# x laid out turned for the first projection, its first slab worked unit by unit over three row tiles, x's rows loaded from GpSimd's queue

## The chip, the cores and the metric

The kernel runs on one core of a Trainium2 chip. A core has TensorE (PE in the profile), VectorE (DVE), ScalarE (ACT), GpSimd (POOL) and the sync engine (SP), each with its own instruction order, and 16 DMA engines that they share. The metric is the device time of one execution in microseconds (us); lower is better.

## What is computed

Two transformer blocks follow each other on x of 512 rows and 1024 columns, all in float32. Only the head of the first block matters here:

```python
xn = rmsnorm(x, attn_norm_g)                  # x / sqrt(mean(x*x) + eps) * g, by row
proj = jnp.einsum('bsd,de->bse', xn, w_in)    # 512 x 1024 times 1024 x 2312
qa, ka, va, qb, kb, vb, f_logit = jnp.split(proj, IN_SPLITS, axis=-1)
qa = rmsnorm(qa.reshape(b, s, A_HEADS, HEAD_DIM), q_norm_a)    # each head of 64 on its own
ka = rmsnorm(ka.reshape(b, s, A_KV_HEADS, HEAD_DIM), k_norm_a)
out_a = swa_sinks_attention(qa, ka, va, sink_logits)
...
log_f = jax.nn.log_sigmoid(f_logit + b_forget)
out_b = forgetting_attention(qb, kb, vb, log_f)
mixed = jnp.concatenate([out_a, out_b], axis=-1)
x = x + mixed @ w_out
x = x + jnp.square(jax.nn.relu(rmsnorm(x, mlp_norm_g) @ w_up)) @ w_down
```

The second block (modulated norms, neighbourhood attention, a pooling mixer, another MLP) comes after it and is not touched.

## The kernel before, in words

Every float32 product is made of three TensorE passes in a rounded format: each operand is split into a high part (ScalarE copies it, `w_hi`, `xt_hi`) and the rest (VectorE subtracts, `w_lo`, `xt_lo`), and hi*hi, hi*lo and lo*hi are summed in PSUM. Weights come in slabs of 1024 rows and up to 512 columns, each slab as four units `raw[0]` to `raw[3]` of 256 rows (512 KB at full width). The sync engine loads the units in order (`unit`, `slab`). The next slab's unit q waits until VectorE has split the present one (`unit_split`). `w_hi` and `w_lo` have two slots.

x is in four row tiles m of 128 rows. A product needs x turned, with the 1024 columns on the partitions (`xt_hi`, `xt_lo`, eight k-steps). Before the change row tile m is made so: its rows are loaded (512 KB), ScalarE squares and sums them (`first_squares`) and takes part of the root (`first_root`), VectorE refines the root (`refine`), multiplies the rows by root and gain (`scaled`), TensorE turns them against the identity matrix (`turn_rows`), ScalarE and VectorE split the result (`xt_high`, `xt_low`). Row tile 0 is multiplied by the gain alone, and its root is applied behind the product (`root0`, `late_root`). The gain's row is spread over the partitions by two small products with a row of ones.

`FIRST` is the order of the first eight output tiles g: slab 0 (q of the first attention) for row tiles 0, 1, 2, then slab 1 (k, v and the forget gates, 264 columns) for row tiles 0 to 3, then slab 0 for row tile 3. Tile g is in PSUM bank g % 4. A tile of q or k goes through a chain in which two engines alternate, one tile after the other: ScalarE squares it (`head_squares`), VectorE sums by head (`head_means`), ScalarE takes logarithm and exponential (`head_roots`), VectorE refines and multiplies (`head_rows`, into `qn`; it ends with `gemm_free`, which frees the bank), TensorE turns it (`turn_heads`), and ScalarE stores it with its gain (`head_gain`, into `q_a` or `k_a`, ends with `qk_stored`). In ScalarE's order the four units of slab 2 are split amid the chain of tiles 6 and 7.

Behind tile 7 TensorE makes the first scores (`scores(0)`), which wait for `gemm_free` 6 and `qk_stored` 4, and then tile 8 in pieces of three k-steps (`part_product`), which waits for `gemm_free` 7. From there on, attention and the tiles of slabs 2 to 4 alternate in a written-out order of 70 halves. Everything is ordered by semaphores whose counts are written into the code.

Of the kernel before, what the change touches and what calls it, by code (L numbers as in the profile page):

```python
# [14 lines left out]
P = 128  # L15
D = 1024
# [33 lines left out]
FIRST = ((0, 0), (0, 1), (0, 2), (1, 0), (1, 1), (1, 2), (1, 3), (0, 3))  # L50
N_IN1, N_OUT, N_MLP, N_IN2 = 5, 2, 4 * NCH, 4
# [188 lines left out]
def build(nc, t, out):  # L240
    ctx = ExitStack()
    with ctx:
# [50 lines left out]
        gain_row = at("gain_row", [1, D], F32, H + 28 * K)  # L293
        ones_row = at("ones_row", [1, P], F32, H + 20 * K)
# [37 lines left out]
        gains = place("gains", [P, 4], F32)  # L332
        cvec = place("cvec", [P, 2, KT], F32)
# [14 lines left out]
        gain1 = at("gain1", [P, D], F32, E)  # L348
# [38 lines left out]
        def sem(name):  # L387
# [15 lines left out]
        hi_split, unit_split = sem("hi_split"), sem("unit_split")  # L403
        gemm_done, gemm_free = sem("gemm_done"), sem("gemm_free")
# [10 lines left out]
        row_ready, gain_spread, gain_copied, first_half, gain_copied_act = (sem(n) for n in (  # L415
            "row_ready", "gain_spread", "gain_copied", "first_half", "gain_copied_act"))
# [34 lines left out]
        root0 = st[:, 3, STAT_N1:STAT_N1 + 1]  # L451

        def late_root(m):
            return {"scale": root0} if m == 0 else {}
# [3 lines left out]
        def _(sp):  # L458
            def small(dst, src, s):
                sp.dma_start(dst, src).then_inc(s, 16)  # L460

            def x_tile(m):
                sp.dma_start(x[:, m, :], t["x"][m * P:(m + 1) * P, :]).then_inc(x_loaded[m], 16)

            x_tile(0)
# [10 lines left out]
            def slab(s, w, c0, width):  # L476
                for q in range(UQ):
                    wait = 4 * (s - 1) + q + 1 if s else None
                    unit(q, rows(w, 0, q)[:, :, c0:c0 + width], width, wait)
                    if s == 0 and q == 0:  # L480
                        small(ident[:], t["c_ident"], ident_loaded)
                    if s == 0 and q:
                        x_tile(q)

            for s, (c0, width) in enumerate(IN1_COLS):
                if s == 1:

                    small_loads = (
                        (gains[0:HD, 0:1], t["q_norm_a"].rearrange("(p a) -> p a", a=1), heads_loaded),
                        (gains[HD:P, 0:1], t["q_norm_a"].rearrange("(p a) -> p a", a=1), heads_loaded),  # L490
                        (gains[0:HD, 1:2], t["k_norm_a"].rearrange("(p a) -> p a", a=1), heads_loaded),
                        (gains[HD:P, 1:2], t["k_norm_a"].rearrange("(p a) -> p a", a=1), heads_loaded),
                        (gains[0:HD, 2:3], t["q_norm_b"].rearrange("(p a) -> p a", a=1), heads_loaded),
                        (gains[HD:P, 2:3], t["q_norm_b"].rearrange("(p a) -> p a", a=1), heads_loaded),
                        (gains[0:HD, 3:4], t["k_norm_b"].rearrange("(p a) -> p a", a=1), heads_loaded),
                        (gains[HD:P, 3:4], t["k_norm_b"].rearrange("(p a) -> p a", a=1), heads_loaded),
                        (b_f[:], t["b_forget"].rearrange("(p a) -> p a", a=1), vec_loaded),
                        (sink[:], t["sink_logits"].rearrange("(a n) -> a n", a=1), vec_loaded),
                        (cvec[:, 0, :], t["c"], vec_loaded),
                        (cvec[:, 1, :], t["c_ctx"], vec_loaded),  # L500
                        (identb[:], t["c_identb"], vec_loaded),
                        (causal[:], t["c_causal"], vec_loaded),
                        (edge[:], t["c_edge"], vec_loaded),
                        (pscale[:], t["pool_scale"], vec_loaded),
                        (negsel[:].rearrange("h g p -> h (g p)"), t["c_negsel"], negsel_loaded),
                    )
                    for q in range(UQ):
                        src = rows(t["w_in"], 0, q)
                        for args in small_loads[5 * q:5 * (q + 1)]:
                            small(*args)  # L510
                        sp.wait_ge(unit_split, q + 1)
                        sp.dma_start(raw[q][:, :, 0:256], src[:, :, c0:c0 + 256]).then_inc(raw_loaded[q], 16)
                        sp.dma_start(raw[q][:, :, 256:KV_W], src[:, :, 2304:2312]).then_inc(raw_loaded[q], 16)
                else:
                    slab(s, t["w_in"], c0, width)
# [40 lines left out]
        def _(pool):  # L556
# [4 lines left out]

            pool.wait_ge(unit_split, 4 * (SLAB_OUT2 + 1))
# [21 lines left out]
        def _(act):  # L584
# [15 lines left out]
            load(gain_row[:], t["attn_norm_g"].rearrange("(a n) -> a n", a=1), gain1_loaded)  # L600
# [42 lines left out]
            first_squares(0)  # L643
            high_of(0, 0)
            first_root(STAT_N1)
            xt_high(NT_1, 0, halves=[0])
            high_of(0, 1)
            xt_high(NT_1, 0, halves=[1])
            first_squares(1)
            high_of(0, 2)  # L650
            act.wait_ge(gain_spread, 2)
            did(act.activation(gain1[:, NC:D], gp[3][:], ACT.Copy), gain_copied_act)
            first_root(STAT_N1 + 1)
            high_of(0, 3)
# [11 lines left out]
            def head_squares(g):  # L666
# [6 lines left out]
                if g == 0:  # L673
                    act.wait_ge(rs_done, 4)
                did(act.activation(qsq[:, 0:heads * HD], banks[in_bank(g)][:, 0:heads * HD], ACT.Square,
                                   **late_root(m)), hsq_done)
# [8 lines left out]
            first_squares(2)  # L685
            xt_high(NT_1 + 1, 1)
            first_root(STAT_N1 + 2)
            high_of(1, 0)
            high_of(1, 1)
            first_squares(3)  # L690
            head_squares(0)
            xt_high(NT_1 + 2, 2)
            first_root(STAT_N1 + 3)
            head_roots(0)
            high_of(1, 2)
            high_of(1, 3)
            xt_high(NT_1 + 3, 3)
            head_squares(1)
            head_roots(1)

            act.wait_ge(xr_ready, 4)
            load(alibi[:], t["c_alibi"], alibi_loaded)

            act.wait_ge(heads_loaded, 16 * 8)

            for g, (s, m) in list(enumerate(FIRST))[2:]:
                if g >= 3:
                    head_gain(g - 3)
# [8 lines left out]
                if s == 1:  # L717
                    did(act.activation(v_a[:, m, :], gp[g % 4][:, P:2 * P], ACT.Copy, **late_root(m)), v_copied)
# [361 lines left out]
        def _(pe):  # L1080
# [1364 lines left out]
```

## Time and profile before

| | before |
|---|---|
| median of 3 runs | 1186.05 us (1185.82 to 1186.39) |
| the profiled execution, its own time | 1186.4 us |
| its span in the trace | 1184.5 us |
| TensorE busy | 1167.0 us (99%) |
| VectorE, ScalarE, GpSimd busy | 706.3, 476.1, 24.8 us |
| mean granted TensorE clock | 0.998 |
| DMA | 144.28 MB, mean 122 GB/s |

All times in the trace count from the start of the span. TensorE's busy time is nearly the whole span, so the views of the first 55 us say more than the shares: there the timeline gives each instruction's start and length, and what the engine had waited for. A matmul is shown about 0.39 us long for 512 columns, while the next starts 0.23 us later: they are pipelined.

### The profile page before, as it was taken

The numbers are of one execution on the slowest core, as the hardware profiler recorded it, in microseconds if no ns is written. First come the engines' busy times: TensorE is split into PE (matmuls) and PEld (weight loads), VectorE is DVE, ScalarE is ACT, GpSimd is POOL, SyncE is SP. The second block draws the span as 40 slices with busy tenths as digits, with TensorE's granted clock in tenths as the row PEclk, the third lists the DMA queues.
The fourth block names the chain that finished last, engine by engine and source line by source line (L and its number), as shares of the span: only waits on it lengthen the run. The fifth ranks groups of instructions, "written<-read, shape, count | busy, mean of one in ns | idle before, by whom it ended". The sixth has DMA issues, their size and how long they took to land.

```text
span 1184.5 us, 16596 instructions
## 1 busy us (share of the span) xinstructions
PE 1167.0 (99%) x6158; PEld 946.1 (80%) x6160; DVE 706.3 (60%) x1084; ACT 476.1 (40%) x858; POOL 24.8 (2%) x23
## 2 busy tenths in 40 slices
PE   8999999989999999999999999999999999999997
PEld 5877776688888888888888886678988888888886
DVE  7786567768787786842788235747633333324335
ACT  6655344545234234324541114845631532432431
POOL 0000000000000000000000004300000000000000
PEclk9999999999999999999999999999999999999999
DMA  7322211218766676734425111222333322323301
GB/s 229 125 72 71 72 36 54 73 52 271 243 224 242 215 254 206 232 125 142 143 72 171 72 72 46 80 101 72 128 99 96 105 91 89 110 85 99 117 16 71
DMA packets 77533, 144.28 MB, mean 122 GB/s; under 512 B 8339, under 2 KB 12307, under 8 KB 77460
## 3 DMA queue, kind: packets, MB, share of 16 engines
q1 hardware_dynamic: 54882, 99.12, 24.7%
q10 hardware_dynamic: 22578, 44.18, 11.4%
q8 instruction: 46, 0.75, 0.3%
q14 instruction: 27, 0.22, 0.1%
HBM read 140.36 MB, written 2.13 MB: 120 GB/s over the span
## 4 chain that ended last, share of the span: by engine, by line
PE 91%; DVE 5%; ACT 2%; issue 2%; DMA 0%; DVEq 0%; ACTq 0%
PE gemm L1091 26%; PE gemm L1093 25%; PE gemm L1092 25%; PE aux L1132 1%; PE aux L1338 1%; PE gemm L1378 1%; PE gemm L1380 1%; PE gemm L1379 1%; DVE nmax L2199 1%; PE aux L1091 1%; PE gemm L1275 1%; PE aux L1093 1%; PE aux L1092 1%; PE gemm L1288 1%; PE aux L1617 1%
## 5 line engine op out<-in xcount | busy, mean ns | idle before, releaser
L1091 PE MATMUL gemm<-xt_hi,w_hi 128*128 128x512 f32 (+1 forms) x704 | 254.4, 361 | 1.3 <-issue 1.1
L1093 PE MATMUL gemm<-xt_hi,w_lo 128*128 128x512 f32 (+1 forms) x704 | 253.6, 360 | 0.0
L1092 PE MATMUL gemm<-xt_lo,w_hi 128*128 128x512 f32 (+1 forms) x704 | 253.5, 360 | 0.0
L1707 DVE TENSOR_TENSOR w_lo<-w_raw,w_hi 128x1024 fp32r<-128x1024 f32 (+1 forms) x176 | 208.0, 1210 | 35.1 <-ACT w_hi L842 30.4
L842 ACT ACTIVATE w_hi<-w_raw 128x1024 fp32r<-128x1024 f32 x124 | 124.1, 1050 | 211.4 <-PE gemm L1093 132.9
L1091 PE MATMUL gemm<-w_hi,ht_hi 128*128 128x512 f32 (+1 forms) x512 | 198.9, 388 | 0.0
L1093 PE MATMUL gemm<-w_hi,ht_lo 128*128 128x512 f32 (+1 forms) x512 | 198.4, 387 | 0.0
L1092 PE MATMUL gemm<-w_lo,ht_hi 128*128 128x512 f32 (+1 forms) x512 | 198.4, 387 | 0.0
L1091 PEld LDWEIGHTS gemm<-xt_hi,w_hi 128*128 128x128 f32 x704 | 132.7, 188 | 21.9 <-issue 1.7
L1093 PEld LDWEIGHTS gemm<-xt_hi,w_lo 128*128 128x128 f32 x704 | 132.7, 189 | 20.1
L1092 PEld LDWEIGHTS gemm<-xt_lo,w_hi 128*128 128x128 f32 x704 | 132.7, 188 | 19.8
L2005 DVE TENSOR_TENSOR ht_lo<-hid,ht_hi 128x512 fp32r<-128x512 f32 x64 | 44.3, 692 | 162.4 <-ACT hid L855 162.4
L1093 PEld LDWEIGHTS gemm<-w_hi,ht_lo 128*128 128x128 f32 x512 | 96.1, 188 | 19.7
L1092 PEld LDWEIGHTS gemm<-w_lo,ht_hi 128*128 128x128 f32 x512 | 96.2, 188 | 19.5
L1091 PEld LDWEIGHTS gemm<-w_hi,ht_hi 128*128 128x128 f32 x512 | 96.1, 188 | 19.4
L850 ACT ACTIVATE relu<-gemm 128x512 f32<-128x512 f32 x64 | 38.2, 597 | 165.3 <-PE gemm L1093 160.2
L2062 DVE SCALAR_TENSOR_TENSOR mod_acc<-wm,csil,mod_acc 128x512 f32<-128x512 f32 x112 | 84.1, 751 | 5.8 <-DMA wm<-in_w_mod 1.5
L1091 PE MATMUL gemm<-w_hi,xt_hi 128*128 128x512 f32 (+1 forms) x208 | 80.2, 386 | 0.4 <-DVE xt_lo L1697 0.4
L1093 PE MATMUL gemm<-w_hi,xt_lo 128*128 128x512 f32 (+1 forms) x208 | 77.9, 374 | 0.0
L1092 PE MATMUL gemm<-w_lo,xt_hi 128*128 128x512 f32 (+1 forms) x208 | 77.6, 373 | 0.0
L606 ACT ACTIVATE w_hi<-w_raw 128x1024 fp32r<-128x1024 f32 (+1 forms) x52 | 51.0, 1021 | 61.1 <-PE gemm L1093 60.0
L2019 DVE TENSOR_TENSOR sub<-sub,gemm 128x512 f32<-128x512 f32 (+1 forms) x24 | 16.2, 676 | 60.5 <-PE gemm L1093 60.5
(268 smaller groups left out, 1385.8 us busy)
## 6 DMA issues: line engine op xcount, KB each, us to landing
wm<-in_w_mod ACTq DMA_DIRECT2D x64, 512.0 KB, 4.7
w_raw<-in_w_in SPq DMA_DIRECT2D x32, 512.0 KB, 4.3
w_raw<-in_w_up SPq DMA_DIRECT2D x32, 512.0 KB, 3.9
w_raw<-in_w_down SPq DMA_DIRECT2D x32, 512.0 KB, 5.7
w_raw<-in_w_mlp_in SPq DMA_DIRECT2D x32, 512.0 KB, 3.6
w_raw<-in_w_mlp_out SPq DMA_DIRECT2D x32, 512.0 KB, 4.4
w_raw<-in_w_out SPq DMA_DIRECT2D x16, 512.0 KB, 4.0
x<-in_x SPq DMA_DIRECT2D x4, 512.0 KB, 6.5
```

The source lines that it names most:

```text
L606: act.activation(w_hi[slot(s)][:, UK * q:UK * (q + 1), 0:width], raw[q][:, :, 0:width], ACT.Copy).then_inc(hi_split, 1)
L842: act.activation(w_hi[s % 2][:, UK * q:UK * (q + 1), :], raw[q][:, :, :], ACT.Copy).then_inc(hi_split, 1)
L850: act.activation(relu[c % 2][:], gp[(t0 + c) % 4][:], ACT.Relu).then_inc(relu_done, 1)
L1091: pe.matmul(bank, lh, rh, start=(k == 0), stop=False)
L1092: pe.matmul(bank, lh, rl, start=False, stop=False)
L1093: mm = pe.matmul(bank, ll, rh, start=False, stop=(k == KT - 1))
L1132: mm = pe.transpose(dst, src, ident[:])
L1275: pe.matmul(bank[e][:, lo:256], q_a[rows[e], h // 2, n * P:(n + 1) * P], k_a[rows[e], swap, (n - 1) * P + lo:(n + 1) * P], start=True, sto ...
L1707: dve.tensor_tensor(w_lo[slot(s)][:, ks, 0:width], raw[q][:, :, 0:width], w_hi[slot(s)][:, ks, 0:width].bitcast(F32), ALU.subtract).then_i ...
L2005: dve.tensor_tensor(ht_lo[:, c, :], hid[c % 2][:], ht_hi[:, c, :].bitcast(F32), ALU.subtract).then_inc(hid_lo, 1)
L2019: dve.tensor_tensor(cols, cols, bank[:], ALU.add).then_inc(gemm_free, 1)
L2062: ins = dve.scalar_tensor_tensor(acc, w, c, acc, ALU.mult, ALU.add)
```

## The change

x is given to the kernel a second time, laid out turned (`x_turned`, 128 partitions, 8 k-steps, 512 tokens), and the gain with it by partition. ScalarE's queue loads it in five transfers, ScalarE makes `xt_hi` straight from it (`x_high`: a copy with the gain as scale, all four row tiles at once) and VectorE `xt_lo` (`x_low`). The root of every row tile, not only the first, is applied behind the products (`root1`). The transposes of x and the two gain products are gone. Slab 0 is worked unit by unit for row tiles 0, 1 and 2 together (`first_products`); its first unit is loaded and split in halves. The sync engine's queue has slab 0's units, then slab 1's, then the small loads, then slab 2's. The rows of x, which the sums of squares and the later residual need, are loaded from GpSimd's queue once the first half unit is split (`first_split`). ScalarE computes all four row statistics between slab 0's and slab 1's splits, and tile 0's chain waits for the last of them (`rs_done` 8). Small constants that were 17 transfers are now 10.

```diff
-            x_tile(0)
...
+            def first_unit():
+                c0, width = IN1_COLS[0]
+                for k in range(UK):
+                    sp.dma_start(raw[0][:, k, 0:width], t["w_in"][k * P:(k + 1) * P, c0:c0 + width]
+                                 ).then_inc(first_loaded if k == 0 else raw_loaded[0], 16)
...
+            pool.wait_ge(first_split, 1)
+            for m in range(TT):
+                pool.dma_start(x[:, m, :], t["x"][m * P:(m + 1) * P, :]).then_inc(x_loaded[m], 16)
...
+            load(gain1[:], t["attn_norm_g"], gain1_loaded)
+            for k in range(UK):
+                load(x_turned[:, k, :], t["x_turned"][:, k, :], first_turned if k == 0 else turned_loaded[0])
+            for q in range(1, UQ):
+                load(x_turned[:, UK * q:UK * (q + 1), :], t["x_turned"][:, UK * q:UK * (q + 1), :], turned_loaded[q])
...
+            def x_high(k):
+                act.wait_ge(*x_arrived(k))
+                did(act.activation(xt_hi[:, k, :], x_turned[:, k, :], ACT.Copy, scale=gain1[:, k:k + 1]), xt_hi_done)
...
+            for q in range(1, UQ):
+                x_high(UK * q)
+                x_high(UK * q + 1)
+                high_of(0, q)
+            for m in range(TT):
+                first_squares(m)
+                if m:
+                    first_root(STAT_N1 + m - 1)
+                high_of(1, m)
+            first_root(STAT_N1 + TT - 1)
...
                 if g == 0:
-                    act.wait_ge(rs_done, 4)
+                    act.wait_ge(rs_done, 2 * TT)
...
-            for g, (s, m) in list(enumerate(FIRST))[2:]:
-                if g >= 3:
-                    head_gain(g - 3)
+            for g, (s, m) in enumerate(FIRST):
+                if g == 4:
+                    act.wait_ge(heads_loaded, 16)
+                if g >= 4:
+                    head_gain(g - 4)
...
+            def first_products():
+                def step(m, k, lhs, w):
+                    return pe.matmul(gp[m][:], lhs[:, k, m * P:(m + 1) * P], w[slot(0)][:, k, :],
+                                     start=(lhs is xt_hi and w is w_hi and k == 0), stop=(w is w_lo and k == KT - 1))
...
-                if g >= 3:
-                    if g == 3:
-                        pe.wait_ge(xt_lo_done, 2 * TT)
-                    turn_heads(g - 3)
+                if g == 4:
+                    pe.wait_ge(ident_loaded, 16)
+                if g >= 4:
+                    turn_heads(g - 4)
...
+            first_products()
+            split_ready(1)
+            for g, (s, m) in list(enumerate(FIRST))[FIRST_ROWS:]:
+                width = KV_W if s == 1 else NC
+                product(g, gp[g % 4], tokens(xt_hi, xt_lo, m), w_cols(s, width), width, wait_free=g >= 4,
+                        mid=lambda: between(g), mid_k=5 if s == 1 else 3)
+            turn_heads(4)
...
+            for m in range(TT):
+                mean_square(STAT_N1 + m, STAT_N1 + m + 1)
+                if m:
+                    refine(STAT_N1 + m - 1)
+                low(1, m)
+            refine(STAT_N1 + TT - 1)
...
-            for g in range(2, PHASE - 1):
+            for g in range(PHASE - 1):
                 head_means(g)
...
                 head_rows(g)
+                if g == 4:
+                    sinks()
```

The first place is ScalarE's order between slab 0's last split and the first two tiles' chains. `w_hi_54` is slab 0's slot, `w_hi_53` slab 1's, `junk,st<-x` the sum of squares of a row tile, `qsq` the squares of a tile. Before, from its last split of slab 0 on:

```order
L606 ACTIVATE w_hi_54<-w_raw_52 128x1024 [waits raw_loaded3,rs0_done]
L620 ACTIVATE junk,st<-x 128x1024 [waits x_loaded2]
L636 ACTIVATE xt_hi<-aux 128x4x128 [waits xr_turned,ssq_done]
...
L606 ACTIVATE w_hi_53<-w_raw_49 128x2x264 [waits raw_loaded0,rs0_done]
L606 ACTIVATE w_hi_53<-w_raw_50 128x2x264 [waits raw_loaded1]
L620 ACTIVATE junk,st<-x 128x1024 [waits x_loaded3]
L675 ACTIVATE qsq<-gemm,st 128x512 [waits rs_done,gemm_done,ssq_done]
```

And after:

```order
L644 ACTIVATE xt_hi<-x_turned,gain_126 128x512 [waits turned_loaded3,xt_hi_done]
L604 ACTIVATE w_hi_54<-w_raw_52 128x1024 [waits raw_loaded3,xt_hi_done]
L618 ACTIVATE junk,st<-x 128x1024 [waits x_loaded0]
L604 ACTIVATE w_hi_53<-w_raw_49 128x2x264 [waits raw_loaded0,ssq_done]
...
L618 ACTIVATE junk,st<-x 128x1024 [waits x_loaded3]
L623 ACTIVATE st<-st 128x1 [waits ms_done,ssq_done]
L624 ACTIVATE st<-st 128x1 [waits ln_done]
L604 ACTIVATE w_hi_53<-w_raw_52 128x2x264 [waits raw_loaded3,rs0_done]
L623 ACTIVATE st<-st 128x1 [waits ms_done]
L624 ACTIVATE st<-st 128x1 [waits ln_done]
L587 DMA alibi<-in_c_alibi 128x2048 [waits rs0_done]
L683 ACTIVATE qsq<-gemm,st 128x512 [waits rs_done,gemm_done]
```

The first squares of a tile now stand behind all four row statistics and all four splits of slab 1; before, two of those splits and one statistic's root came after them.

The second place is TensorE's order from the last k-step of tile 7 to tile 8. `aux<-ident,qn` are the transposes of a finished tile, `gemm<-k_a,q_a` are scores, `w_hi_53` is slab 2's slot by now. Before:

```order
L1093 MATMUL gemm<-w_hi_54,xt_lo 128x512
L1275 MATMUL gemm<-k_a,q_a 128x128 [waits alibi_loaded,silu_step,vec_loaded,qk_stored,ones_ready,gemm_free]
L1275 MATMUL gemm<-k_a,q_a 128x128
L1278 MATMUL gemm<-alibi,identb 128x128
L1279 MATMUL gemm<-sink_rows,ones_full 128x1
...
L1091 MATMUL gemm<-w_hi_53,xt_hi 128x512 [waits unit_split,gemm_free]
```

And after:

```order
L1085 MATMUL gemm<-w_hi_54,xt_lo 128x512
L1204 MATMUL aux<-ident,qn_97 128x128 [waits qk_stored,gemm_free]
L1204 MATMUL aux<-ident,qn_97 128x128
L1268 MATMUL gemm<-k_a,q_a 128x128 [waits alibi_loaded,silu_step,vec_loaded,qk_stored,ones_ready,gemm_free]
L1268 MATMUL gemm<-k_a,q_a 128x128
...
L1083 MATMUL gemm<-w_hi_53,xt_hi 128x512 [waits unit_split,gemm_free]
```

The turning of tile 4 has moved from inside tile 7 to behind it, since every `turn_heads` comes one tile later.

## Rows read from the trace of the kernel before

**Rows 1.** The page: busy time by engine; the chain that ended last.

```profile
PE 1167.0 (99%) x6158; PEld 946.1 (80%) x6160; DVE 706.3 (60%) x1084; ACT 476.1 (40%) x858; POOL 24.8 (2%) x23
PE 91%; DVE 5%; ACT 2%; issue 2%; DMA 0%; DVEq 0%; ACTq 0%
```

**Rows 2.** Waits of TensorE over the span: us in total, times, longest us.

```profile
PE gemm L1148 <- DMA gain_row<-in_attn_norm_g: 3.3, 1, 3.3
PE gemm L1162 <- DVE w_lo L1707: 1.4, 3, 0.9
```

**Rows 3.** Timeline of TensorE: start, length, line; tile 1, first scores, tile 8.

```profile
19.03 0.50 PE L1091 MATMUL gemm<-w_hi,xt_hi 128*128 128x512 f32 x1 [0.36 <-DVE xt_lo L1697]
51.20 0.49 PE L1275 MATMUL gemm<-k_a,q_a 64*128 64x128 f32 x4
51.80 0.47 PE L1091 MATMUL gemm<-w_hi,xt_hi 128*128 128x512 f32 x1
```

**Rows 4.** Transfers of x: issue ns, first and last start us; us to landing.

```profile
L463 SPq DMA_DIRECT2D x<-in_x x4: 396/470/523, 0.7 to 5.5; - x4
DMA to landing us min/median/max: 3.8/6.5/9.0
```

**Rows 5.** Timeline of VectorE: slab 1's split, refining, and the chain of the tiles.

```profile
20.83 1.33 DVE L1707 TENSOR_TENSOR w_lo<-w_raw,w_hi 128x528 fp32r<-128x528 f32 x2
24.64 0.27 DVE L1674 TENSOR_SCALAR st<-st 128x1 f32<-128x1 f32 x1
33.78 0.16 DVE L1776 CAST sink_parts<-sink 1x8 bf16<-1x8 f32 x1
35.45 0.69 DVE L1735 TENSOR_REDUCE hst<-qsq 128x8 f32<-128x512 f32 x1
38.32 0.28 DVE L1735 TENSOR_REDUCE hst<-qsq 128x2 f32<-128x128 f32 x1
50.25 0.62 DVE L1751 TENSOR_TENSOR qn<-gemm,hst 128x128 f32<-128x128 f32 x2
```

**Rows 6.** Groups of 0 to 27 us by shape: count, busy us, mean ns.

```profile
L606 ACT ACTIVATE w_hi<-w_raw 128x1024 fp32r<-128x1024 f32 x4 | 4.2, 1057 | 0.4 <-DMA w_raw<-in_w_in 0.3
L1132 PE MATMUL aux<-ident,xr 128*128 128x128 f32 x24 | 4.2, 331 | 0.2 <-DVE xr L1686 0.2
L636 ACT ACTIVATE xt_hi<-aux 128x512 fp32r<-128x512 f32 x6 | 3.6, 595 | 1.9 <-PE aux L1132 1.8
```

**Rows 7.** Windows: busy us by engine, granted clock, DMA share, GB/s; loading, the end.

```profile
10.00:11.00 1.00, 1.00 (x5) 0.86 (x5) 0.50 (x1) 0.97 (x2) 0.00 (x0) 1.00 1.02 406
1177.00:1178.00 1.00, 0.95 (x8) 0.75 (x7) 0.71 (x3) 0.51 (x2) 0.00 (x0) 1.00 0.92 342
1181.00:1181.50 0.50, 0.00 (x0) 0.00 (x0) 0.47 (x2) 0.00 (x0) 0.00 (x0) 0.50 0.00 0
```

**Rows 8.** Timeline of ScalarE: a row statistic, slab 1's split, a root, squares of tiles.

```profile
14.62 1.04 ACT L620 ACTIVATE junk<-x 128x1024 bf16<-128x1024 f32 x1
15.57 0.18 ACT L620 ACTIVATION_READ_ACCUMULATOR junk<-x 128x1 f32 x1
18.24 1.18 ACT L606 ACTIVATE w_hi<-w_raw 128x528 fp32r<-128x528 f32 x2
22.87 0.20 ACT L625 ACTIVATE st<-st 128x1 f32<-128x1 f32 x1
20.49 0.69 ACT L675 ACTIVATE qsq<-gemm,st 128x512 f32<-128x512 f32 x1
45.92 0.28 ACT L675 ACTIVATE qsq<-gemm 128x128 f32<-128x128 f32 x1
```

**Rows 9.** Chain of waits: start, length; turnings inside tiles 4 and 5, tile 7.

```profile
33.85 0.44 PE aux L1207 x4
37.20 0.44 PE aux L1207 x4
45.53 0.23 PE gemm L1091
```

More of the change, by code:

```diff
@@ L448, in rpb_part, with root1 @@
             return rpb_run[64 * b:64 * b + 64, h, :], src
-        root0 = st[:, 3, STAT_N1:STAT_N1 + 1]
-        def late_root(m):
-            return {"scale": root0} if m == 0 else {}
+        def root1(m):
+            return st[:, 3, STAT_N1 + m:STAT_N1 + m + 1]
         @block_fn(nc, ctx, "sync")
@@ L479, in slab @@
                     unit(q, rows(w, 0, q)[:, :, c0:c0 + width], width, wait)
[L480 to L515, printed above, removed]
@@ new lines, in first_unit @@
+            def first_unit():
[3 more added lines that the diff above has]
+                                 ).then_inc(first_loaded if k == 0 else raw_loaded[0], 16)
+            first_unit()
+            for q in range(1, UQ):
+                unit(q, rows(t["w_in"], 0, q)[:, :, IN1_COLS[0][0]:IN1_COLS[0][0] + IN1_COLS[0][1]], IN1_COLS[0][1], None)
+            for q in range(UQ):
+                src, c0 = rows(t["w_in"], 0, q), IN1_COLS[1][0]
+                sp.wait_ge(unit_split, q + 1)
+                sp.dma_start(raw[q][:, :, 0:256], src[:, :, c0:c0 + 256]).then_inc(raw_loaded[q], 16)
+                sp.dma_start(raw[q][:, :, 256:KV_W], src[:, :, 2304:2312]).then_inc(raw_loaded[q], 16)
@@ new lines, in _ @@
+            small(gains[:], t["head_gains"], heads_loaded)
+            small(ident[:], t["c_ident"], ident_loaded)
+            small(b_f[:], t["b_forget"].rearrange("(p a) -> p a", a=1), vec_loaded)
+            small(sink[:], t["sink_logits"].rearrange("(a n) -> a n", a=1), vec_loaded)
+            small(cvec[:], t["c_both"], vec_loaded)
+            small(identb[:], t["c_identb"], vec_loaded)
+            small(causal[:], t["c_causal"], vec_loaded)
+            slab(2, t["w_in"], *IN1_COLS[2])
@@ L516, in _ @@
+            small(edge[:], t["c_edge"], vec_loaded)
+            small(pscale[:], t["pool_scale"], vec_loaded)
+            small(negsel[:].rearrange("h g p -> h (g p)"), t["c_negsel"], negsel_loaded)
+            for s, (c0, width) in list(enumerate(IN1_COLS))[3:]:
+                slab(s, t["w_in"], c0, width)
             for half in range(2):
@@ L1142, in turn_rows @@
                     turn_half(n, half, permute)
-            pe.wait_ge(row_ready, 1)
-            pe.wait_ge(gain1_loaded, 16)
-            for half in range(2):
-                pe.matmul(gp[2 + half][:], ones_row[:], gain_row[:, half * NC:(half + 1) * NC],
-                          start=True, stop=True).then_inc(gain_spread, 1)
-            pe.wait_ge(ident_loaded, 16)
-            pe.wait_ge(first_half, 1)
-            turn_half(NT_1, 0)
-            pe.wait_ge(xr_ready, NT_1 + 1)
-            turn_half(NT_1, 1)
```

247 lines of the change are left out of this document (106 added, 141 removed).

## The prediction

> **What bounds the kernel now.** I read the page first: TensorE is busy for 99% of the span and holds 91% of the chain that ended last [rows 1]. So only TensorE's idle time and its extra work can be won. Then the waits of TensorE: the longest are in the first 20 us, 3.3 us for the gain and 1.4 us for splits of slab 0 [rows 2]. The timeline shows tile 1 starting at 19.03 and TensorE gapless from about 21 us: the first scores come at 51.20, tile 8 at 51.80 [rows 3]. The change alters everything up to tile 8 and, beyond it, only a few scale operands off the path. If TensorE stays the bound behind tile 8, the whole effect is the shift of tile 8's start. That start waits for `gemm_free` 7, the end of tile 6's chain. The reader is to see in the timeline of VectorE that this came at 50.25 + 0.62 = 50.87 [rows 5], 0.93 us ahead of tile 8. So the chain that alternates between ScalarE and VectorE was nearly as long as TensorE's own work. A change that starts it late makes it the bound.
>
> **What is removed from TensorE.** 24 transposes of x take 4.2 us and the last 8 about 1 us [rows 6], and the gain products and the first waits go too. The same 72 matmuls of tiles 0 to 2 and the five other tiles remain. Alone this would give some 5 us. The question is whether anything else lets TensorE use it.
>
> **Step 1, when slab 0 is all there.** Before, eight units of 512 KB (four of x, four of slab 0) came in one queue. The first landed at 0.74 + 3.8 = 4.5 us, the last at 5.5 + 9.0 = 14.5 [rows 4]: 1.43 us a unit, small transfers between them. At 406 GB/s a unit is 1.29 us [rows 7]. I take 1.35, so that k units land at 3.15 + 1.35 k. After, `x_turned` and slab 0 are again eight units, 13.95 us if nothing else moves. But x's rows, four more units, start once the first half of slab 0's unit 0 is split: one unit's worth of data at 4.5, `x_high` 0.6 to 0.7 [rows 6], the half split 0.6, so 5.9, and with the issue (SP's take 0.47 [rows 4]) about 6.4. The DMA share there is already 1.02 [rows 7], so x's rows can only take from the others. No transfer of GpSimd stands in the trace. The bounds are 13.95 (x's rows take nothing before the end) and 3.15 + 12 x 1.35 = 19.35 (all twelve land together). I take equal shares of three queues: 2.4 units are there at 6.4, the other 5.6 need 5.6 x 1.35 x 1.5 = 11.3 us, hence 17.75.
>
> The full DMA share at 10 us says that transfers side by side slow each other. The Trainium skill, "DMA: Bandwidth & Descriptors", section "Queues, rings and completion order", has each DMA engine go round the queues that have work, a packet at a time. By that rule x's rows do take their share, and the sum stays as it is; if they took nothing, it would be the 13.95 case. No run here shows three queues at once.
>
> **Step 2, ScalarE before tile 0's chain.** Behind the last landing ScalarE has two `x_high` and the split of unit 3 (2 x 0.7 + 1.06 [rows 6], 2.5 us with gaps): 20.2. Then four statistics of 1.04 + 0.18 (1.18 by starts), four roots of two 0.20 instructions (0.46), four splits of slab 1 at 0.6 [rows 8]: 8.96 us. It can't run ahead: the order is fixed, and the first squares of a tile wait for all four roots. The last split ends at 28.7, VectorE's half takes 0.7, refining two instructions, 0.5 [rows 5]: tile 0's squares start at Z = 30.1. Before they started at 20.49 [rows 8]. This is the main loss.
>
> **Step 3, the chain from Z to tile 8.** The first squares take 0.69 [rows 8], then three tiles of 512 columns at 2.87 us (35.45 to 38.32 [rows 5]); with 0.06 each for the multiply that now applies the root, an estimate, VectorE reaches tile 3 at Z + 9.6. From there to tile 6's squares it was 38.32 to 45.92, 7.6 us [rows 5, 8]. To it come `sinks`, 33.78 to 35.45 = 1.67 [rows 5], which now stands behind tile 4; some 0.4 of it fall into VectorE's waiting, 1.3 count. Scaled forms cost 0.69 - 0.60 = 0.09 [rows 6, 8] on squares and two copies of two tiles, 0.5. A store of q stands where one of k did, 0.2 as an estimate. That is Z + 19.2. Tile 6's squares to the end of its chain took 45.92 to 50.87, 4.95 [rows 5, 8], with 0.1 for the root and 0.1 to TensorE: tile 8 at Z + 24.4 = 54.5. The scores' other wait, tile 3's store, ends sooner, about Z + 23.1.
>
> **TensorE beside it.** Unit 3 is split at 21.5, its 18 matmuls at 0.23 end at 25.7. Slab 1 is ready at Z - 0.5 = 29.6, so TensorE idles 3.9 us. Tile 4 waits for tile 0's chain, Z + 3.8; three tiles with turnings at 3.35 (33.85 to 37.20) and tile 7 at 5.7 (45.53 to 51.20) [rows 3, 9] plus the turning behind it end at Z + 19.9. TensorE then idles some 3.3 us and starts scores at Z + 23.2. So it isn't the bound.
>
> **At nothing.** `x_low` and the splits on VectorE (10 us of work in 17) hide behind the loads; if the loads came at 13.95 they would still be done within 1.5 us of them. The gain, identity and head gains land long before use; without that cover tile 4's turning would wait. The alibi load is issued while ScalarE waits for the last refining. Fewer small transfers free SP, which waits for splits anyway. Slab 2's units land during the chain.
>
> **The sum.** Tile 8 at 54.5 against 51.8 is +2.7 us. The profiled execution took 1186.4, so 1189.1; the median of the runs stands 0.35 below it: 1188.8. With step 1's bounds tile 8 comes at 50.75 or 56.15, which is -1.05 or +4.35, so 1185.0 to 1190.4.
>
> **Rivals.**
> Rival A, x's rows don't hold up the others: GpSimd's queue starts late or yields. For it: nothing in the trace shows that queue. Against it: the full DMA share. Then the units land at 13.95, Z is 26.4, tile 8 at 50.75: 1185.0. Chance 0.25.
> Rival B, the chain isn't the bound and TensorE is: it ends faster. The chain would have to run ahead of the order that I read, since its pace in the trace may contain slack from TensorE (tile 2's reducing came behind `sinks`). Tile 8 would then start at Z + 20.5. It decides once the chain takes under 20.5 us from Z instead of 24.4. With Z = 26.4 that is 46.9, -4.9 us: 1181.1. Against it: tiles 3 to 5 each kept to 2.5 to 2.9 us without waiting for TensorE. Chance 0.12.
> Rival C, the clock: the two idle stretches of 3.9 and 3.3 us let TensorE's clock fall to 1.2 GHz. For it: at the end, after the last matmul at about 1178, the granted clock was 0.50 by 1181 [rows 7], some 3 us of idling. Against it: the first matmul, after 3.3 us without any, ran at full rate. The first stretch costs nothing (TensorE isn't the bound). The second would halve the clock over the scores (0.6 us) and the first nine matmuls of tile 8 (2.1 us): from 0 to 5.5 us (the whole tile), I take 2.7, so 1191.5. Chance 0.18.
> The Trainium skill, "TensorE: Matmul & The Clock Gate", Part 1, says that the throttled state is the default and that activity releases it. The trace's end agrees (0.50), its start doesn't. By that rule rival C would hold.
>
> **How the numbers follow.** The forecast has 0.45, A 0.25, B 0.12, C 0.18. A measurement of this kernel tells 0.2% from no change, 2.4 us: 1183.7 to 1188.4. Faster: all of B with a tight chain, 0.12. Same: A, and 0.10 of the forecast (GpSimd's first transfer a us or more late brings it under +2.4). Slower: the other 0.35 and C, 0.53. The range takes in A below and most of C above: 1184.3 to 1191.3; the forecast alone 1187.6 to 1190.4.
>
> **What would show it.** Step 1: the last of `w_raw` or `x_turned` lands near 17.8 rather than 14. Step 2: ScalarE gapless from the last split of slab 0 for 9 us, tile 0's squares at about 30. Step 3: tile 6's multiply ends 24.3 us behind those squares, TensorE's wait before the first scores names ScalarE's store of k. C: a granted clock under 1.00 in windows after 53 us. I am wrong if TensorE has no idle stretch of over 2 us before the scores, if tile 8 starts before 51, or if the behaviour behind tile 8 differs by more than a us.

## The result, and the profile after

The changed kernel takes 1190.1 us (median of 6 runs, 1189.3 to 1190.6) where the kernel before takes 1186.0 (6 runs): ratio 1.0035, 95% interval 1.0024 to 1.0045. It is slower by 4.1 us. The forecast was +2.7 us to 1188.8. In a second session it was +3.5 us (1.0030, 1.0019 to 1.0042).

The waits of TensorE in the profile after, which answer to [rows 2] (us in total, times, longest):

```profile
PE gemm L1141 <- ACT w_hi L649: 7.6, 1, 7.6
PE gemm L1268 <- ACT k_a L669: 3.2, 1, 3.2
PE gemm L1083 <- DVE w_lo L1699: 2.6, 1, 2.6
```

The first product waits until 7.55; slab 1's first product waits 2.6 us for its last split; the first scores wait 3.2 us for the store of k. The gain's wait of 3.3 us is gone, and so are the transposes of x.

The timeline of ScalarE after, from the last split of slab 0 to tile 0's squares (start, length; in brackets the idle time before and what ended it):

```profile
17.64 1.06 ACT L604 ACTIVATE w_hi<-w_raw 128x1024 fp32r<-128x1024 f32 x1 [0.48 <-DMA w_raw<-in_w_in]
...
21.30 0.65 ACT L604 ACTIVATE w_hi<-w_raw 128x528 fp32r<-128x528 f32 x1 [1.55 <-DMA w_raw<-in_w_in]
21.85 1.04 ACT L618 ACTIVATE junk<-x 128x1024 bf16<-128x1024 f32 x1
...
27.85 0.64 ACT L604 ACTIVATE w_hi<-w_raw 128x528 fp32r<-128x528 f32 x1
...
29.78 0.69 ACT L683 ACTIVATE qsq<-gemm,st 128x512 f32<-128x512 f32 x1 [0.95 <-DVE st L1667]
```

The last line is Z of the prediction, the start of tile 0's squares; before, it was 20.49 [rows 8]. Between slab 0's last split and slab 1's first ScalarE waits 1.55 us for slab 1's unit 0. From the start of that first split of slab 1 to Z it takes 8.48 us: four splits, three statistics, the roots, and 0.95 us of waiting for the last refining.

The chain then runs as before, in VectorE's timeline: tile 3's reduce, `sinks`, tile 5's reduce behind it, and tile 6's norm (they answer to [rows 5]).

```profile
39.48 0.29 DVE L1734 TENSOR_REDUCE hst<-qsq 128x2 f32<-128x128 f32 x1
...
45.06 0.16 DVE L1773 CAST sink_parts<-sink 1x8 bf16<-1x8 f32 x1
...
46.73 0.29 DVE L1734 TENSOR_REDUCE hst<-qsq 128x2 f32<-128x128 f32 x1
...
50.76 2.36 DVE L1699 TENSOR_TENSOR w_lo<-w_raw,w_hi 128x1024 fp32r<-128x1024 f32 x2 [0.60 <-ACT w_hi L604]
...
53.62 0.74 DVE L1748 SCALAR_TENSOR_TENSOR qn<-gemm,st,hst 128x128 f32<-128x128 f32 x2
```

TensorE's timeline around tile 8 (answers to [rows 3]):

```profile
49.67 0.38 PE L1204 MATMUL aux<-ident,qn 128*128 128x128 f32 x2
53.28 0.49 PE L1268 MATMUL gemm<-k_a,q_a 64*128 64x128 f32 x4 [3.23 <-ACT k_a L669]
...
54.41 0.79 PE L1083 MATMUL gemm<-w_hi,xt_hi 128*128 128x512 f32 x1 [0.39 <-DVE qn L1748]
55.00 0.63 PE L1084 MATMUL gemm<-w_lo,xt_hi 128*128 128x512 f32 x1
55.43 0.63 PE L1085 MATMUL gemm<-w_hi,xt_lo 128*128 128x512 f32 x1
...
57.82 0.39 PE L1085 MATMUL gemm<-w_hi,xt_lo 128*128 128x512 f32 x1
...
60.65 0.49 PE L1268 MATMUL gemm<-k_a,q_a 64*128 64x128 f32 x4
```

Tile 8 starts at 54.41 instead of 51.80: +2.61. Its matmuls start 0.43 us apart up to 57.5, where the kernel before has 0.23 throughout. The windows show the clock (answers to [rows 7]; busy time of the five engines, granted clock, DMA share, GB/s):

```profile
30.00:34.00 4.00, 4.00 (x22) 4.00 (x22) 2.80 (x9) 1.57 (x4) 0.00 (x0) 0.57 0.94 283
54.00:58.00 4.00, 3.61 (x11) 2.82 (x10) 3.86 (x7) 2.07 (x5) 0.00 (x0) 0.57 0.89 275
```

So behind each of the two idle stretches (2.6 and 3.2 us) TensorE ran at 1.2 GHz for some 3 to 4 us. The first costs nothing: TensorE is ahead of the chain there, with 3.2 us to spare before the scores. In the second, the ninth matmul of tile 8 starts 3.41 us behind the first; where the clock stays at 1.00 (E10 below) it is 1.95 us. That is 1.46 us. 2.61 + 1.46 = 4.07: the second scores start at 60.65, in the kernel before at 56.57, and the spans differ by as much (1188.6 - 1184.5 = 4.1). Nothing is lost or won behind them.

### The profile page after: what moved, and what is told of

Read it like the earlier page. It is cut to its first block, busy times and chain, and to the rows that moved or that the text cites. A ratio compares the mean times of both kernels' runs of the same rounds, so it can differ in the third digit from the quotient of the medians.

```text
span 1188.6 us, 16514 instructions
## 1 busy us (share of the span) xinstructions
PE 1163.0 (98%) x6124; PEld 945.7 (80%) x6124; DVE 702.4 (59%) x1078; ACT 478.5 (40%) x858; POOL 27.0 (2%) x27
## 3 DMA queue, kind: packets, MB, share of 16 engines
q1 hardware_dynamic: 53682, 97.02, 24.4%
## 4 chain that ended last, share of the span: by engine, by line
PE 88%; DVE 6%; ACT 2%; issue 2%; DMA 1%; ACTq 0%; DVEq 0%; SPq 0%
PE gemm L1083 25%; PE gemm L1085 25%; PE gemm L1084 24%; PE aux L1331 1%; PE aux L1124 1%; PE gemm L1371 1%; DMA w_raw<-in_w_in 1%; PE gemm L1373 1%; PE gemm L1372 1%; DVE nmax L2180 1%; PE aux L1083 1%; PE aux L1610 1%; PE aux L1085 1%; PE aux L1084 1%; PE gemm L1281 1%
## 5 line engine op out<-in xcount | busy, mean ns | idle before, releaser
L1083 PEld LDWEIGHTS gemm<-w_hi,ht_hi 128*128 128x128 f32 x512 | 96.1, 188 | 19.4
L1083 PE MATMUL gemm<-w_hi,xt_hi 128*128 128x512 f32 (+1 forms) x192 | 75.3, 392 | 3.0 <-DVE w_lo L1699 2.6
L1085 PE MATMUL gemm<-w_hi,xt_lo 128*128 128x512 f32 (+1 forms) x192 | 72.8, 379 | 0.0
L1084 PE MATMUL gemm<-w_lo,xt_hi 128*128 128x512 f32 (+1 forms) x192 | 72.6, 378 | 0.0
```

What stands on the lines that cost most here:

```text
L1083: pe.matmul(bank, lh, rh, start=(k == 0), stop=False)
L1084: pe.matmul(bank, lh, rl, start=False, stop=False)
L1085: mm = pe.matmul(bank, ll, rh, start=False, stop=(k == KT - 1))
```

## The experiments

Each run was timed in turn with the kernel before on the same chip (medians of before 1186.0 in the first session, 1186.4 to 1186.5 in the others). Times are therefore compared by their ratios to it, and "by the ratios" below means a difference of two ratios times 1186 us. Z, tile 8 and the tail come from one profiled execution each, whose own time can lie beside the median: e1's, e3's and e5's were 0.9 us faster than their medians, e6's 1.9 us slower. "Tail" is the span less tile 8's start: 1132.7 before.

| kernel | time, us | ratio to before, 95% | Z | tile 8 | tail |
|---|---|---|---|---|---|
| changed, first session | 1190.1 | 1.0024 to 1.0045 | 29.78 | 54.41 | 1134.2 |
| e9 changed again | 1189.9 | 1.0019 to 1.0042 | 29.41 | 54.02 | 1134.1 |
| e1 sinks first | 1188.7 | 1.0009 to 1.0027 | 29.62 | 52.91 | 1133.1 |
| e2 matmuls as filler | 1189.6 | 1.0016 to 1.0036 | 29.56 | 54.53 | 1133.1 |
| e3 chain early | 1187.8 | 1.0000 to 1.0018 | 23.76 | 51.12 | 1134.0 |
| e4 x rows by SyncE | 1189.8 | 1.0018 to 1.0039 | 28.97 | 53.60 | 1134.3 |
| e5 splits spread | 1188.8 | 1.0011 to 1.0030 | 28.78 | 51.86 | 1134.2 |
| e10 e2 and e4 | 1189.3 | 1.0015 to 1.0033 | 29.44 | 54.06 | 1133.1 |
| e11 statistics first | 1188.8 | 1.0011 to 1.0029 | 26.23 | 51.33 | 1135.2 |
| e6 e1, e5, better e3 | 1182.4 | 0.9953 to 0.9978 | 25.11 | 48.39 | 1134.1 |
| e7 e6, x by SyncE | 1182.2 | 0.9950 to 0.9977 | 23.54 | 46.70 | 1134.4 |
| e8 e6, warmed | 1183.5 | 0.9966 to 0.9986 | 23.99 | 47.27 | 1134.4 |

**E9: the changed kernel again**, no edit.

> The changed kernel itself once more, to have it beside the kernel before in the same session as other runs, since the edits compared here are worth 1 to 3 us each. Theory: the same +4 us (1.0035), of which 2.6 is the later start of tile 8 and 1.4 the halved clock in its first matmuls. Rival (part of the +4.1 belonged to that one session): under +3 us.

Measured +3.5 us. From Z to tile 8 it took 24.61 us, in the first session 24.63, in e4 24.63, in e10 24.62. With this order the chain behind Z had one length; Z itself differs by 0.4 us between the two profiles of the same kernel, so a smaller difference in Z tells nothing.

**E1: sinks first**

```diff
+            pool.dma_start(sink[:], ...).then_inc(sink_loaded, 16)
             pool.wait_ge(first_split, 1)
...
+            sinks()
             dve.wait_ge(gain1_loaded, 16)
             x_low(0)
...
-                if g == 4:
-                    sinks()
```

> The sink logits are loaded by GpSimd ahead of x's rows and `sinks` runs first of all on VectorE, beside the loads, instead of behind tile 4's norm. Theory (the chain of ScalarE and VectorE from Z sets tile 8): tile 5's reduce came at 46.73 behind `sinks` (45.06 to 46.73) where ScalarE's squares were done at 45.3, so 1.3 us leave the chain; tile 8 starts near 53.1 instead of 54.41 and the time falls from 1190.1 to about 1188.8 (1187.4 if with the shorter idle time TensorE's clock stays up as well). Rival (something else, TensorE's own work or the weights of slab 2, holds tile 8): tile 8 stays within 0.3 us of 54.4 and the time within 0.4 of 1190.1.

From Z to tile 8 it took 52.91 - 29.62 = 23.29 us, 1.34 less than in the changed kernel: the 1.3 of step 3. TensorE idled 0.6 us before the scores instead of 3.2: the scores came 1.5 us earlier, and tile 7 ended 1.1 us later, since behind the first idle stretch the low clock lasted longer here (the turning behind tile 7 at 50.77, not 49.67). The clock stayed at 1.00 in tile 8.

```profile
51.78 0.49 PE L1269 MATMUL gemm<-k_a,q_a 64*128 64x128 f32 x4 [0.64 <-ACT k_a L670]
...
52.91 0.50 PE L1084 MATMUL gemm<-w_hi,xt_hi 128*128 128x512 f32 x1 [0.39 <-DVE qn L1764]
53.25 0.40 PE L1085 MATMUL gemm<-w_lo,xt_hi 128*128 128x512 f32 x1
53.48 0.39 PE L1086 MATMUL gemm<-w_hi,xt_lo 128*128 128x512 f32 x1
```

The profiled execution was 2.6 us faster than the changed kernel's (1.5 for tile 8, 1.1 for the tail). The median, 1188.7, is by the ratios 2.0 us (first session of the changed kernel) or 1.4 (second) below it.

**E2: filler before the scores**

```diff
             turn_heads(4)
+            pe.wait_ge(qk_stored, 2)
+            for i in range(13):
+                pe.matmul(aux[1][:], xt_hi[:, i % KT, 0:P], xt_hi[:, i % KT, :], start=True, stop=True)
```

> 13 matmuls of 512 columns, whose result nobody reads, go to TensorE between tile 4's turning and the first scores, 13 x 0.23 = 3.0 us of the 3.2 us that it idles there. Theory (rival C of the prediction: idling lets the clock fall to 1.2 GHz, which costs 1.4 us in tile 8's first seven matmuls): granted clock 1.00 from 50 to 60 us, tile 8's matmuls at 0.23 from 54.4 on, the time about 1188.7. Rival (the slow matmuls come from something else that begins there, such as slab 2's loads or first splits): pitch still 0.43, time 1190.1 or above.

TensorE's timeline of e2:

```profile
50.76 3.24 PE L1223 MATMUL aux<-xt_hi 128*128 128x512 f32 x13
...
54.53 0.48 PE L1083 MATMUL gemm<-w_hi,xt_hi 128*128 128x512 f32 x1
54.84 0.40 PE L1084 MATMUL gemm<-w_lo,xt_hi 128*128 128x512 f32 x1
55.08 0.39 PE L1085 MATMUL gemm<-w_hi,xt_lo 128*128 128x512 f32 x1
```

Same start of tile 8 within 0.12 us, same loads and splits beside it, but matmuls 0.23 us apart: the idle stretch was the cause of the slow matmuls, not what begins there. The tail is 1.1 us shorter, not 1.46. In e1 and e10, whose tails are the same, the second scores wait 0.4 us for ScalarE's `prob_a`, which makes up the rest; in e2 no such wait stands out, and 0.4 us stay unexplained. By the ratios e2 is 1.1 us below the changed kernel's first session and 0.5 below its second; 1.4 was forecast.

**E3: the chain early.** Tile 0's squares wait for the first root alone; slab 1's splits come ahead of the statistics of row tiles 2 and 3, which go into the chains of tiles 0 and 1. VectorE's order follows.

```diff
-            for m in range(TT):
-                first_squares(m)
-                if m:
-                    first_root(STAT_N1 + m - 1)
-                high_of(1, m)
-            first_root(STAT_N1 + TT - 1)
...
-                    act.wait_ge(rs_done, 2 * TT)
+                    act.wait_ge(rs_done, 2)
...
+            first_squares(0)
+            first_squares(1)
+            first_root(STAT_N1)
+            high_of(1, 0)
...
+            head_squares(0)
+            high_of(1, 3)
+            head_roots(0)
+            first_squares(2)
+            first_root(STAT_N1 + 2)
+            head_squares(1)
```

> Tile 0's squares wait for the root of row tile 0 alone; the statistics of row tiles 2 and 3 go behind them, into ScalarE's waits within the chains of tiles 0 and 1, and slab 1's splits ahead. Nothing else is changed. Theory (the main loss is step 2, four statistics between slab 0 and the chain): Z falls from 29.8 to about 24.5, slab 1 is split by about 26.5 and TensorE no longer idles 2.6 us behind slab 0. The chain keeps its 24.6 us and takes in 1 us of the statistics: tile 8 near 50, time about 1185.5, or 1184.5 if the clock stays up before it. Rival (the x rows or slab 1's units land too late to use it): Z near 28 and the time over 1188.

Z fell by 6 us to 23.76, and TensorE no longer waited for slab 1. But Z to tile 8 grew to 27.36, and tile 8 came at 51.12, not 50; the clock still fell behind an idle stretch of 4.2 us. The time, 1187.8, misses the forecast of 1185.5 too; by the ratios it is 2.5 to 3.1 us below the changed kernel. Of the extra 2.7 us, 1 was forecast for the statistics that now stand in the chain. One place of the rest is in ScalarE's timeline: the root of row tile 2 waited for its mean, which stood behind tile 0's norm on VectorE, and tile 1's squares stood behind that root.

```profile
27.15 0.18 ACT L618 ACTIVATION_READ_ACCUMULATOR junk<-x 128x1 f32 x1
28.34 0.20 ACT L623 ACTIVATE st<-st 128x1 f32<-128x1 f32 x1 [1.00 <-DVE st L1669]
28.57 0.20 ACT L624 ACTIVATE st<-st 128x1 f32<-128x1 f32 x1
28.81 0.69 ACT L677 ACTIVATE qsq<-gemm,st 128x512 f32<-128x512 f32 x1
```

**E4: x's rows by SyncE**

```diff
-            for m in range(TT):
-                pool.dma_start(x[:, m, :], ...).then_inc(x_loaded[m], 16)
...
+            for m in range(TT):
+                sp.dma_start(x[:, m, :], ...).then_inc(x_loaded[m], 16)
             for q in range(UQ):
                 src, c0 = rows(t["w_in"], 0, q), IN1_COLS[1][0]
```

> x's four row transfers are issued by SyncE behind slab 0's units and ahead of slab 1's, not by GpSimd; this undoes that part of the change alone. Theory (step 1: equal shares of three queues hold slab 0 up to 17.75 us): slab 0 and x_turned are complete near 14 to 15 us and the last split of slab 0 ends near 16.5 instead of 18.7, but x's rows land from about 15 to 19.4 and slab 1's first unit at about 20; Z near 28.6, tile 8 near 53.2, time about 1189. Rival (x's rows take nothing from the others; TensorE's 72 matmuls, not the loads, end at 26.8 by themselves): landings of slab 0 within 0.5 us of those with GpSimd's queue, time within 0.4 of 1190.1.

ScalarE's timeline of e4: the last split of slab 0, the first of slab 1, Z.

```profile
16.64 1.06 ACT L602 ACTIVATE w_hi<-w_raw 128x1024 fp32r<-128x1024 f32 x1
...
20.48 0.65 ACT L602 ACTIVATE w_hi<-w_raw 128x528 fp32r<-128x528 f32 x1 [1.74 <-DMA w_raw<-in_w_in]
...
28.97 0.69 ACT L681 ACTIVATE qsq<-gemm,st 128x512 f32<-128x512 f32 x1 [0.96 <-DVE st L1665]
```

The last split of slab 0 began at 16.4 to 16.6 in the three kernels with SyncE's issue (e4, e7, e10) and no longer waited for a transfer. With GpSimd's issue it began at 17.2 to 19.2 in eight profiles, at 16.5 in one (e11). So x's rows seem to hold slab 0 up, in most profiles by some 1 us; more can't be read from this, since ScalarE's own work sets the last split once the unit is there. Z gained little (28.97, where 28.6 was forecast): ScalarE waited 1.74 us instead of 1.55 for slab 1's unit 0. Wherever ScalarE waited for that unit it began its split at 20.3 to 21.3, with either queue; the same twelve units stand ahead of it in both. The time is the changed kernel's within the intervals.

**E11: the statistics ahead of slab 1's splits**

```diff
             for m in range(TT):
                 first_squares(m)
                 if m:
                     first_root(STAT_N1 + m - 1)
-                high_of(1, m)
             first_root(STAT_N1 + TT - 1)
+            for m in range(TT):
+                high_of(1, m)
```

> On the changed kernel, ScalarE and VectorE do all four statistics first and then the four splits of slab 1, instead of one split behind each; no wait is changed. Theory (ScalarE's work between slab 0 and Z doesn't start at the last split of slab 0, but at the landing of slab 1's unit 0, 8.48 us before Z in each run so far): the statistics fill the 1.5 us for which ScalarE waited there. From 18.6 four squares and roots of 1.67 us, 6.7, and four splits of 0.55, 2.2, give Z = 27.5 instead of 29.4 to 29.8, tile 8 near 52.1 and the time 2.0 to 2.2 us below the changed kernel, about 1188. Rival (ScalarE was held by the order of its work alone, from the last split of slab 0 on): Z moves by under 0.5 us, the time stays near 1190.

Z came at 26.23, 1.3 us before its forecast of 27.5, mainly since slab 0's last split began at 16.51 in this run; there was no wait for a transfer behind it:

```profile
16.51 1.06 ACT L604 ACTIVATE w_hi<-w_raw 128x1024 fp32r<-128x1024 f32 x1
17.48 1.04 ACT L618 ACTIVATE junk<-x 128x1024 bf16<-128x1024 f32 x1
...
24.63 1.70 ACT L604 ACTIVATE w_hi<-w_raw 128x528 fp32r<-128x528 f32 x3
26.23 0.67 ACT L684 ACTIVATE qsq<-gemm,st 128x512 f32<-128x512 f32 x1
```

In all seven profiles with the changed kernel's order here (itself, e1, e2, e4, e5, e9, e10), Z is the first split of slab 1, at 20.30 to 21.30, plus 8.48 or 8.49 us. In all seven ScalarE had waited for that unit, 0.91 to 2.42 us, however early slab 0 was done (16.44 in e10, 18.06 in e2): its landing set Z. E11 takes the wait away, and Z comes 3.2 us before e9's. Not all of that is the wait: about 1.5 us is, 1.0 us is the wait for the last refining, which now passes beside slab 1's splits, and 0.8 us is the earlier last split of slab 0. From Z to tile 8 it took 25.10 us, 0.5 more than before, since all four of VectorE's splits of slab 1 (2.56 us from 24.82) now stand directly before tile 0's reduce. Tile 8 started 3.1 us earlier than in the changed kernel's first profile, but 3.4 us of idling before the scores cost the clock for 11 matmuls this time, not 7, and the tail is the longest of all, 1135.2. By the ratios the gain is 1.2 us on the second session and 1.8 on the first, below the 2.0 to 2.2 of the forecast.

**E5: slab 2's first splits out of tile 6's chain**

```diff
+                if g == 5:
+                    high_of(2, 0)
                 if g == 6:
-                    high_of(2, 0)
                     high_of(2, 1)
...
                 if g == 6:
                     low(2, 0)
-                    low(2, 1)
                 head_rows(g)
+                if g == 6:
+                    low(2, 1)
```

> Slab 2's first two units, whose splitting stands within tile 6's chain (ScalarE 2.0 us, VectorE 2.36 us), are spread: ScalarE splits unit 0 within tile 5's chain and unit 1 within tile 6's, VectorE does unit 0 within tile 6's and unit 1 behind tile 6's norm. Chain theory: tile 6's chain loses some 2 us, tile 5's gains some 0.5, so tile 8 starts near 52.9 instead of 54.4 and the time is about 1188.6, a us less if TensorE's clock stays up. Rival (tile 8 then waits for its own second unit, which is split behind the norm): a wait of over a us in tile 8's third matmul, time 1189.5 or more.

Z to tile 8 took 23.08 us, 1.55 less, and tile 8's matmuls did not wait for the second unit. The clock fell behind 2.2 us of idling. The median, 1188.8 us, is near the 1188.6 that was expected. Tile 8 came a us earlier than forecast (51.86 against 52.9), because Z was 28.78 in this profile, whose time was 0.9 us under the median.

**E10: e2's filler and e4's issue together**, the two edits shown above.

> x's rows issued by SyncE (e4) and the 13 matmuls before the first scores (e2) together, on the changed kernel. If the two losses are separate terms, they add: e4 moved tile 8 from 54.4 to 53.6 (0.8 us), e2 kept the clock (behind tile 8's start 1133.1 instead of 1134.2 us to the end of the span, 1.1 us), so 1.9 us below the changed kernel. If they share a cause, little more than the larger, 1.1 us. With TensorE's 13 matmuls the scores may come 0.6 us late; tile 8 near 53.7.

The clock was kept (tail 1133.1), but Z was 29.44, since slab 1's unit 0 landed at 20.96: e4's gain is not there. By the ratios the run is 1.3 us below the changed kernel's first session and 0.7 below its second. So the sum of 1.9 us failed, and with it the reading of e4's 0.8 us as an effect of SyncE's issue: from e4 to e10, which both have that issue, Z differs by 0.5 us.

**E6: e1 and e5, and an e3 without the wait.** Against e3, tile 1's squares come ahead of row tile 2's root, tile 2's squares ahead of row tile 3's root and behind a wait for eight steps of `rs_done`, and VectorE takes each refining behind the next tile's means.

```diff
             first_squares(2)
-            first_root(STAT_N1 + 2)
             head_squares(1)
-            first_squares(3)
+            first_root(STAT_N1 + 2)
             head_roots(1)
+            first_squares(3)
+            act.wait_ge(rs_done, 8)
+            head_squares(2)
             first_root(STAT_N1 + 3)
+            head_roots(2)
```

> Three edits together: `sinks` first (as e1), slab 2's splits spread (as e5), and the early chain of e3 with tile 1's and tile 2's squares no longer behind the statistics of row tiles 2 and 3. By the chain: e3's tile 8 at 51.1, less 1.5 for `sinks`, 1.5 for the splits and 1.1 for the wait at 28.3, gives 47.0. By TensorE alone: in e3 it had done tile 7 and the turning at 45.8, and scores take 0.6, so 46.4. The later of the two, 47.0, is 4.8 before the kernel before (51.8): about 1181.2. Rival (rows behind tile 8 can't use it, since slab 2's later units or VectorE's splits come late): 1183 or more, with new waits of TensorE behind 50 us.

1182.4 us, 0.35% faster than the kernel before and some 7.6 us below the changed kernel, against a forecast of 1181.2. In the profiled execution, the slowest of the six at 1184.25, Z was at 25.11, since slab 0's last split waited 1.5 us for its unit. From Z to tile 8 it took 23.28 us; e3's 27.36 less what e1 and e5 saved is 24.5, so the waits that this order takes out of e3 were worth 1.2. TensorE's waits in e6:

```profile
PE gemm L1156 <- ACT w_hi L650: 7.0, 1, 7.0
PE gemm L1098 <- DVE w_lo L1714: 1.7, 1, 1.7
PE gemm L1283 <- ACT prob_a L742: 1.3, 1, 1.3
PE gemm L1283 <- ACT k_a L664: 0.8, 1, 0.8
```

From 14 to 60 us the granted clock is 1.00 in every window. The new wait of 1.3 us, of the second scores for ScalarE, is where part of the gain goes; the rival named such a wait. The edits of e1 and e5 were not tried on the kernel before. TensorE did not wait for the chain there, so they should bring little, but no run shows it.

**E7: e6 with x's rows by SyncE**; e4's edit on e6.

> e6, with x's rows issued by SyncE behind slab 0 as in e4. Where the chain is the bound, slab 0's earlier landing (0.8 us at Z in e4) gives up to 0.8 us: 1180.5. Rival: now TensorE is the bound (it is gapless from slab 0 to the scores) and its 96 first matmuls end when they did: same as e6 within 0.3 us.

1182.2 us, the same as e6. In the profile tile 8 starts at 46.70, 1.7 us before e6's, but the medians don't show that.

**E8: e6 with a warmed TensorE**

```diff
+                pe.wait_ge(ones_ready, 1)
+                for _ in range(60):
+                    pe.matmul(aux[2][:, 0:P], ones_full[:], ones_full[:], start=True, stop=True)
                 pe.wait_ge(xt_hi_done, 1)
```

> e6, with 60 matmuls of 128 columns, whose result nobody reads, on TensorE before the first product, while it waits for x_turned. In the changed kernel the first 14 matmuls came at a pitch of 0.43 us, the later ones at 0.23, though the records give a granted clock of 1.00 in both. Theory (half the rate follows on idling): pitch 0.23 from the first product on, slab 0's products end near 24 instead of 26.8, and where TensorE bounds the stretch up to tile 8 the time falls by up to 0.7 us below e6. Rival (the first products are slow for another reason, such as operands that come late): pitch still 0.43 until 13 us.

TensorE's first rows in e8, behind them those of the changed kernel, and the first products of the kernel before:

```profile
1.06 5.20 PE L1161 MATMUL aux<-ones_full 128*128 128x128 bf16 x60 [1.06 <-DVE ones_full L1665]
7.02 0.94 PE L1156 MATMUL gemm<-w_hi,xt_hi 128*128 128x512 f32 x3 [0.76 <-ACT w_hi L650]
```

```profile
7.55 1.62 PE L1141 MATMUL gemm<-w_hi,xt_hi 128*128 128x512 f32 x3 [7.55 <-ACT w_hi L649]
8.97 1.48 PE L1141 MATMUL gemm<-w_hi,xt_lo 128*128 128x512 f32 x3
```

```profile
8.87 1.92 PE L1162 MATMUL gemm<-w_hi,xt_hi 128*128 128x512 f32 x4
```

Three matmuls in 0.94 against 1.48 to 1.62: the first products were slow because TensorE had been idle. There is no gain in time (1183.5, 1.1 us above e6 with overlapping intervals): behind the first product TensorE waits 1.2 us in three places for splits and for `xt_lo`, and slab 0's products end at 25.6 us, against 26.1 in e6 and the 24 of the forecast.

## Why the prediction was right, and where it was off

- **The forecast**, +2.7 us to 1188.8, had the direction and its cause right and was 1.3 us short of the 1190.1 measured. The range held, because its upper end had room for rival C. Two of the prediction's own signs went against it: ScalarE was not gapless behind slab 0's last split, and the stretch behind tile 8 differed by more than a us (tail 1134.2 against 1132.7). The sign of rival C, a granted clock under 1.00 after 53 us, came.
- **What bounds it** held. The chain of ScalarE and VectorE sets tile 8; e1, e3, e5, e6 and e11 shorten or advance it, and tile 8 follows while TensorE idles before the scores.
- **Step 1** gave 17.75 for the landing; the last split began at 17.64 behind a transfer. That match is in part luck. GpSimd issued x's rows from 7.72, not 6.4; by the same equal shares the landing would be near 17.1, and in the nine profiles with this issue the last split began anywhere from 16.5 to 19.2. And two `x_high` were not left to do behind it, so slab 0 was split at 18.7, not 20.2.

```profile
7.72 2.26 POOL L554 DMA_DIRECT2D x<-in_x  x4 [7.26 <-ACT w_hi L649]
```

- **Step 2** summed ScalarE's work right and missed a wait: slab 1's unit 0 landed 1.5 us after ScalarE was ready for it. The two errors, 1.5 us each way, cancel by luck in Z, 29.78 against 30.1. What set Z was that landing: ScalarE waited for it in all seven profiles of this order. So the lower bound, slab 0 at 13.95 and all that follows 3.8 us earlier, was wrong as a term, and with it rival A: with x's rows out of slab 0's way (e4, e10) ScalarE's own work from about 10 us on still kept the last split at 16.4 to 16.6, and Z didn't follow even that far.
- **Step 3**: tile 3's reduce at Z + 9.7 (9.6), tile 6's squares at 49.20, Z + 19.4 (19.2), tile 8 at Z + 24.6 (24.4). `sinks` 1.34 (1.3). The one late date and the price of the chain gave +2.61 us for a forecast of +2.7.
- **TensorE beside it**: slab 0's products ended at 26.8, not 25.7, bound by TensorE and not by unit 3, since the first 14 matmuls or so ran at 0.43 us. The idle stretches were 2.6 (3.9) and 3.2 us (3.3).
- **Rival B** fell: TensorE idled 3.2 us before the scores, and the chain took 24.6 us from Z, not 20.5.
- **Rival C** is what the sum lacks. I gave it 0.18 on two grounds. The clock of 0.50 at the end of the span was the right one. The ground against it, a first matmul at full rate, was misread: the products at 8.87 before already came at half rate, four in 1.92 us. The price was too high, 1.46 and not 2.7 us, since the low clock held for seven matmuls and not for nine and the scores. With 1.46, which only the runs give, the sum would have been 1190.3, measured 1190.1.
- The rule of the Trainium skill, "TensorE: Matmul & The Clock Gate", Part 1, that the throttled state is the default and activity releases it, agrees with the changed kernel's start (first products 0.43 us apart behind 7.55 us without a matmul), with e8 and with e2.

Left open: why slab 0's last split began anywhere from 16.5 to 19.2 in profiles of kernels whose loads are issued alike, and how much of the difference between a profiled execution and its median that explains.

## What to carry to other kernels

When a change takes work from the engine that is busiest, look for the chain of the others that ended just ahead of it; here it had 0.9 us of slack, and nine microseconds of statistics and splits in front of it used that up. Take the idle time that a change opens on TensorE with its price at the clock behind it. And date the start of a chain by the last thing it needs, here the next slab's first unit, rather than by the end of the work before.

## What the runs showed of the hardware

- The records give a granted clock of 1.00 from 4 to 14 us in the changed kernel, while 512-column matmuls came 0.43 us apart, half the rate; with 60 small matmuls ahead of them they came 0.23 to 0.28 us apart (e8). Up to about 13 us the pitch of the matmuls told the clock in this kernel, and the column did not:

```profile
10.00:12.00 2.00, 2.00 (x7) 1.52 (x6) 0.88 (x2) 1.48 (x3) 0.00 (x0) 1.00 1.03 411
```

- Idle stretches of 2.2 to 4.2 us before the scores were each followed by a clock of 1.2 GHz (e5, e9, e4, e11, e3), for 5 to 11 matmuls; 0.6 us of idling there (e1) was not, nor the 1.7 us that e6 idled behind slab 0.
- With the DMA share at 1.0, x's rows issued by SyncE instead of GpSimd went with a last split of slab 0 at 16.4 to 16.6 us instead of 16.5 to 19.2. Slab 1's unit 0, behind all of them, was waited for until 20.5 to 21.3 us with SyncE's issue (e4, e10, e7) and until 20.3 to 21.3 with GpSimd's.
